# Attention loop of the mixers: probabilities scaled on GpSimd, one turned tile copied by VectorE

## The reference

```python
def attend_latent(q, k, v, k_ctx, v_ctx):          # 256 own tokens, keys: own + context = 512
    k_all = jnp.concatenate([k, k_ctx], axis=1)
    v_all = jnp.concatenate([v, v_ctx], axis=1)
    def one_block(q_blk):                           # 128 queries
        s = jnp.einsum('bqkgd,bskd->bkgqs', q_blk, k_all).astype(jnp.float32) * ATTN_SCALE
        p = jax.nn.softmax(s, axis=-1).astype(v_all.dtype)
        return jnp.einsum('bkgqs,bskd->bqkgd', p, v_all)

def attend_context(q, k, v):                        # layer 0 only: 256 context tokens and keys
    s = jnp.einsum('bqkgd,bskd->bkgqs', q, k).astype(jnp.float32) * ATTN_SCALE
    p = jax.nn.softmax(s, axis=-1).astype(v.dtype)
    return jnp.einsum('bkgqs,bskd->bqkgd', p, v)

for layer in range(2):
    # x, ctx: feed-forward 1; projections; attention, pooling and Fourier mixers, then w_out;
    # feed-forward 2 (the context's last steps only in layer 0)
```

## Time and profile before

| | |
|---|---|
| median of 3 runs | 2139.98 us |
| span of the profiled execution, first to last instruction | 2137.7 us |
| around the span (median less span) | 2.3 us |
| TensorE busy | 2051.8 us, 96% of the span |
| VectorE busy | 1423.7 us, 67% |
| ScalarE busy | 693.6 us, 32% |
| GpSimd busy | 244.5 us, 11% |
| attention loop of layer 0 | about 989.8 to 1038.2 us |
| attention loop of layer 1 | about 1875.4 to 1907.1 us |

### The profile page before, as it was taken

One profiled execution on the slowest core, in us unless ns is written; L12 is line 12 of the kernel. 1 busy time (PEld: TensorE's weight loads), 2 busy tenths in 40 slices (PEclk: granted clock), 3 DMA queues, 4 the chain that ended last, 5 costly groups with the idle time before them and its releaser, 6 DMA issues.

```text
span 2137.7 us, 31334 instructions
## 1 busy us (share of the span) xinstructions
PE 2051.8 (96%) x13199; PEld 1702.5 (80%) x13199; DVE 1423.7 (67%) x1890; ACT 693.6 (32%) x962; POOL 244.5 (11%) x286
## 2 busy tenths in 40 slices
PE   8999988887999999999999999999999999999998
PEld 7988975554888888896798888889888888877887
DVE  6887553333788598356578758747866863767675
ACT  6554421112421221245532112123221222464453
POOL 1000003321200000400210000030000004010000
PEclk9999999999999999999999999999999999999999
DMA  9646769999666565332136456445645643415664
GB/s 278 208 169 207 238 255 385 413 406 400 198 177 183 151 198 163 102 99 65 40 109 198 140 156 180 123 121 153 190 134 164 183 122 118 138 46 153 172 185 121
DMA packets 384121, 387.14 MB, mean 181 GB/s; under 512 B 18041, under 2 KB 351342, under 8 KB 371566
## 3 DMA queue, kind: packets, MB, share of 16 engines
q1 hardware_dynamic: 355438, 304.31, 44.1%
q0 software_dynamic: 27952, 79.77, 12.1%
q10 hardware_dynamic: 592, 1.05, 0.1%
HBM read 430.68 MB, written 1.05 MB: 202 GB/s over the span
## 4 chain that ended last, share of the span: by engine, by line
PE 84%; DVE 7%; DMA 6%; ACT 2%; issue 1%; SPq 0%; POOL 0%; DVEq 0%; POOLq 0%; ACTq 0%
PE B L2020 22%; PE B L2022 22%; PE B L2021 22%; PE B L2525 6%; DMA WB<-in_w 5%; PE B L2526 3%; PE B L2473 3%; DVE LO L816 2%; PE B L2862 1%; PE B L2507 1%; DVE HF L1195 1%; PE B L2836 1%; PE B L2847 1%; DMA W<-in_w 1%; DVE hL L1183 1%
## 5 line engine op out<-in xcount | busy, mean ns | idle before, releaser
L2020 PE MATMUL B<-hH,HI 128*128 128x512 f32 (+1 forms) x1600 | 566.5, 354 | 4.9 <-DVE hL L1183 2.4
L2021 PE MATMUL B<-hL,HI 128*128 128x512 f32 (+1 forms) x1600 | 558.5, 349 | 0.0
L2022 PE MATMUL B<-hH,LO 128*128 128x512 f32 (+1 forms) x1600 | 558.3, 349 | 0.0
L816 DVE TENSOR_TENSOR LO<-RAW,HI 128x2048 fp32r<-128x2048 f32 (+3 forms) x218 | 443.2, 2036 | 94.2 <-ACT HI L1571 89.3
L1571 ACT ACTIVATE HI<-RAW 128x2048 fp32r<-128x2048 f32 (+3 forms) x218 | 368.6, 1693 | 342.0 <-PE B L2022 282.6
L2020 PEld LDWEIGHTS B<-hH,HI 128*128 128x128 f32 x1600 | 302.3, 189 | 49.7 <-DVE LO L816 5.4
L2022 PEld LDWEIGHTS B<-hH,LO 128*128 128x128 f32 x1600 | 302.3, 189 | 40.2
L2021 PEld LDWEIGHTS B<-hL,HI 128*128 128x128 f32 x1600 | 302.3, 189 | 39.6 <-issue 1.2
L904 DVE SCALAR_TENSOR_TENSOR MACC<-MADW,CS,MACC 128x1024 f32<-128x1024 f32 x224 | 277.5, 1280 | 7.7 <-DMA MADW<-in_ada_w 1.7
L2022 PE MATMUL B<-aH,LO 128*128 128x512 f32 (+1 forms) x605 | 222.9, 368 | 0.0
L2020 PE MATMUL B<-aH,HI 128*128 128x512 f32 (+1 forms) x605 | 222.6, 368 | 0.0
(11 more groups left out here) (425 smaller groups left out, 3163.0 us busy)
## 6 DMA issues: line engine op xcount, KB each, us to landing
RAW<-in_ffn_w_gu SPq DMA_DIRECT2D x176, 512.0 KB, 5.3
MADW<-in_ada_w POOLq DMA_DIRECT2D x128, 512.0 KB, 4.0
W<-in_w SPq DMA_DIRECT2D x31, 1024.0 KB
RAW<-in_w_in SPq DMA_DIRECT2D x60, 512.0 KB, 4.8
WB<-in_w SPq DMA_DIRECT2D x28, 1024.0 KB
RAW<-in_ffn_w_down SPq DMA_DIRECT2D x56, 384.0 KB, 3.7
RAW<-in_ffn_w_down SPq DMA_DIRECT2D x56, 320.0 KB, 4.3
WA<-in_w SPq DMA_DIRECT2D x17, 1024.0 KB
```

The costliest lines, as they stand in the source:

```text
L816: V.tensor_tensor(LO[s][:, :words], RAW[s][:, :words], HI[t.hi[s]][:, :words].bitcast(F32), ALU.subtract).then_inc(lo_done[s], 1)
L2020: mm(o, wh, xh, start=first, stop=False, **more)
L2021: mm(o, wh, xl, start=False, stop=False, **more)
L2022: return mm(o, wl, xh, start=False, stop=last, **more)
```

## The change

Three things are done in both layers' attention loops.

1. The scaling of the probabilities leaves VectorE. A new function `probabilities(l)` on GpSimd waits for the reciprocals of a pair (`qr_ready`), multiplies its two tiles in place, and raises `prob_ready`, for which TensorE's transposes wait as before. VectorE no longer waits for its own reciprocals.
2. The copy of the second head's turned probabilities (bank 3 into T3) leaves ScalarE. VectorE does it at the head of its iteration, ahead of the maxima. It waits for both heads' transposes.
3. TensorE waits for two semaphores in place of one count: `probT_ready` of ScalarE and `turned_ready` of VectorE, ahead of the values product and where it reuses the banks.

```diff
+            def probabilities(l):
+                t.n["qr_ready"] += 3 if l == 0 else 2
+                for n, (h, q0, k0, nk) in enumerate(attention_pairs(l)):
+                    pool.wait_ge(E["qr_ready"], t.next("qr_ready"))
+                    for c in range(2):
+                        e = PROBS[2 * n % 6 + c][:, :nk]
+                        i = 4 + 2 * n % 4 + c
+                        ins = nc.gpsimd.tensor_scalar(e, e, SM2[:, i:i + 1], None, ALU.mult)
+                    ins.then_inc(E["prob_ready"], 1)
...
             mod_weights(units[1], units[1] + 2)
+            probabilities(0)
             even_squares_in_turn()
...
             after_ffn(2)
+            probabilities(1)
             even_squares(1)
...
                 for u in range(len(pairs) + 3):
                     i = 2 * u % 4
+                    if u >= 3:
+                        h, q0, k0, nk = pairs[u - 3]
+                        ve.wait_ge(E["probT_done"], t.next("probT_done", 2))
+                        V.tensor_copy(T[3][:, :nk], B[3][:, :nk]).then_inc(E["turned_ready"], 1)
...
                         ve.wait_ge(E["exp_ready"], t.next("exp_ready", 2))
-                        link(V.reciprocal(ri, sums))
-                        for c in range(2):
-                            e = PROBS[2 * (u - 1) % 6 + c][:, :nk]
-                            ins = V.tensor_scalar(e, e, ri[:, c:c + 1], None, ALU.mult)
-                        ins.then_inc(E["prob_ready"], 1)
+                        V.reciprocal(ri, sums).then_inc(E["qr_ready"], 1)
...
-                        for c in range(2):
-                            got("probT_done")
-                            A.activation(T[2 + c][:, :nk], B[2 + c][:, :nk], ACT.Copy).then_inc(E["probT_ready"], 1)
+                        got("probT_done")
+                        t.next("probT_done")
+                        A.activation(T[2][:, :nk], B[2][:, :nk], ACT.Copy).then_inc(E["probT_ready"], 1)
...
-                            claim(2 + c, "probT_ready", before + 2 * (u - 3) + c + 1)
+                            claim(2 + c, *(("probT_ready", before + u - 2), ("turned_ready", before_turned + u - 2))[c])
...
-                        pe.wait_ge(E["probT_ready"], t.next("probT_ready", 2))
+                        got("probT_ready")
+                        got("turned_ready")
                         claim(4, "mix_ready")
```

More of the change, by code:

```diff
@@ L1469, in mixers @@
                 pairs = attention_pairs(l)
+                if l == 0:
+                    t.n["probT_done"] += HEADS
                 for u in range(len(pairs) + 3):
                     i = 2 * u % 4
+                    if u >= 3:
+                        h, q0, k0, nk = pairs[u - 3]
+                        ve.wait_ge(E["probT_done"], t.next("probT_done", 2))
+                        V.tensor_copy(T[3][:, :nk], B[3][:, :nk]).then_inc(E["turned_ready"], 1)
                     if u < len(pairs):
@@ L2827, in mixers @@
                 pairs = attention_pairs(l)
-                before = t.n["probT_ready"]
+                if l == 0:
+                    t.n["turned_ready"] = QUADS
+                t.n["qr_ready"] += len(pairs)
+                before, before_turned = t.n["probT_ready"], t.n["turned_ready"]
                 for u in range(len(pairs) + 3):
```

## The result

The changed kernel takes 2154.14 us (median of 5 runs, 2153.7 to 2155.9) against 2139.98 (2139.85 to 2141.91 in 5 runs). The ratio is 1.0064, 95% interval 1.0053 to 1.0075: slower, by some 14 us, well beyond the 0.2% that a measurement tells. The forecast was 2141.1 and the range ended at 2149.0.

The account below looks back on a forecast made before the run. TensorE's own work was taken as the bound; terms 1.04 + 1.08 + 0.40 - 1.44 = +1.1 us turned the span of 2137.7 into 2138.8, with the median 2.3 above it: 2141.1 us. The range was 2139.3 to 2149.

Parts of the forecast that it names:

- What bounds the kernel, and the room of 2.46 us: Steady 512-key loop: TensorE's own work bounds; from reciprocals to transposes 2.46 us, so GpSimd scalings up to 1.12 us are free.
- The scaling on GpSimd: what one costs: One GpSimd scaling in the attention loops: 0.66 us for 512 columns, 0.42 for 256, from AFFINE_SELECT; upper end 1.29.
- Term 1, the first pair: Start of each layer's loop: transposes wait for GpSimd's two scalings, 0.52 us later per layer, +1.04 us.
- Term 2, the copy on VectorE: Values products without long scores before them: VectorE's copy allows T+2.04 against T+1.83, T being the transposes' start; +1.08 us.
- Term 3, 256 keys: 256-key iterations: VectorE's copy puts the values product at T+1.27 against T+1.22, 0.05 for each of eight pairs, +0.40 us.
- Term 4, the low part sooner: VectorE without scaling writes the low part right after the reciprocals, removing TensorE's waits for it; -1.44 us.
- The sum: Both attention loops: 1.04 + 1.08 + 0.40 - 1.44 = +1.1 us, giving 2141.1 us.
- The first: Rival: GpSimd's scaling bounds the loops from 1.12 us; at 1.29 us 2146.3 us, at 1.6 +12.6, at 2.0 +22.6; chance 0.21.
- The mutual blocking: Rival: VectorE and GpSimd hold each other up in the loops; +4.2 us over the forecast, 2145.3 us; chance 0.05.
- The quick handovers: Rival: freed engines win more than handovers cost in the loops; sum -0.2 to -0.8 us, down to 2139.2; chance 0.10.

Follow-up runs that it names:

- f9: Kernel before, scaling still on VectorE, with GpSimd running scaling, product and copy forms on unused tiles from layer 0's loop on; one run, 2143.3 us.
- f6: The whole change, but GpSimd scales by a product with the reciprocal's column broadcast; ratio to before 1.0005, both loops 81.47 us against 80.11.
- f8b: The whole change plus two filler matmuls on TensorE ahead of each layer's first transposes; ratio to before 1.0051, both loops 92.23 us.
- f7: Kernel before, but GpSimd scales only each layer's first pair, one signal after its two tiles; ratio to before 1.0036, both loops 87.25 us.
- f8: The whole change plus five filler matmuls on TensorE ahead of each layer's first transposes; ratio to before 1.0072, both loops 95.13 us.
- g10: Kernel before, but VectorE writes the low part ahead of the scaling; ratio to before 0.9992, both loops 78.43 us against 80.11.
- f1: Kernel before, only the scaling moved to GpSimd, one signal for a pair's two tiles; ratio to before 1.0063, both loops 93.67 us.
- e1: Kernel before, only the scaling moved to GpSimd, with a signal after every tile; ratio to before 1.0035, both loops 87.82 us.
- e7: Kernel before, but GpSimd scales only each layer's first pair, with a signal after every tile; ratio to before 1.0016, both loops 83.16 us.

## Why the prediction was wrong

*What bounds the kernel, and the room of 2.46 us.* Right. With 1.04 us for a scaling the beats are 3.11, with 1.56 they are 3.50. The rule (each 512-key beat grows by t - 1.12) gives +0.44 at 1.56; measured is +0.39.

*"The scaling on GpSimd: what one costs".* This step failed: 0.66 us was put for an instruction that takes 1.56, and 1.12 is where GpSimd begins to decide. I took 0.66 us from AFFINE_SELECT because it has the scaling's traffic, one read and one write. Runs f9 and f6 show that traffic isn't what GpSimd's time goes by here: 1.67 us with a column, 1.62 with a constant, 1.09 with two inputs, all over the same 512 columns. With the product's 1.04 us in its place, 13.2 of the 14.54 us are gone. The upper bound of 1.29 was no bound, since no row had this form. The Trainium skill, "GPSIMD Engine Reference", section Key points, gave an estimate of 0.88 by its factor of two; measured is 3.5 times VectorE's 0.44, so rule and estimate were both too low.

*Term 1, the first pair.* Its form was right. With t = 1.56 it gives 0.52 + 2 x 0.90 = 2.32 us later per layer (measured 2.27 and 2.24), with 1.04 it gives 1.28 (measured 1.16 and 1.17 in f6). What was missing from the whole text is what TensorE's clock does after such an idle time: +4.17 us in the first beats, of which later beats give 0.5 back (f8b: 3.66 net). It is shown by f7, where nothing else is changed, and by f8 and f8b, where the fillers keep the clock up.

*Term 2, the copy on VectorE: +1.08.* Too high. The last pair of layer 1 has the copy at T+1.13 and the values product at T+1.92, not T+2.04 (T+1.83 before). The copy begins 0.08 us sooner than I put it, and the handover takes 0.10, not 0.14 (the row's bracket names ScalarE, whose copy ended at 1919.86; VectorE's ended last, at 1920.39):

```profile
1918.57 1.09 PE L2854 MATMUL B<-MATS,T 128*128 128x128 f32 x8
...
1919.70 0.69 DVE L1490 COPY T<-B 128x512 f32<-128x512 f32 x1 [0.55 <-PE B L2854]
...
1920.49 1.09 PE L2881 MATMUL B<-T,VD 128*64 128x128 f32 x16 [0.83 <-ACT T L1956]
```

*Term 3, 256 keys: +0.40.* Near nothing by itself: the last values product of layer 0 comes at T+1.22 (1043.64 to 1044.86 after), as an undisturbed one did before. f6 stands 3.04 us above g10, 2.33 of it at the start; so by subtraction the terms 2 and 3 were worth 0.7 together, not 1.48.

*Term 4, the low part sooner: -1.44.* Right: -1.68, measured by itself in g10.

*The sum.* With the measured 1.04 us of the product, start +2.33, terms 2 and 3 +0.7, term 4 -1.68: +1.36, the loops of f6 (from which the 0.7 was taken, so this is no test of the sum). That it lies near the forecast's +1.1 is in part luck: at 1.04 us term 1 as recorded gives +2.56 and the whole sum +2.6. What f6 does show is that with a scaling of 1.04 us the kernel stays within the range.

*The rivals.* The first was what happened, at 0.21 the likeliest of the three. Two of its figures don't follow from its own steps. With 0.18 us fixed, 1.6 us means 0.89 at 256 keys: 4.8 for ten beats, 3.8 for the starts, 2.2 for the 256-key beats and the forecast's 1.1 make +11.8, not +12.6; at 2.0 us they make some +18.8, not +22.6. The mechanism without the clock gave 14.54 - 3.66 = 10.9 at 1.56 us, near the +11.8; the whole is above it for lack of the clock. The mutual blocking was no cause here: in layer 0 VectorE's reciprocals have a median of 158 ns beside GpSimd (159 before), with the longest of 16 at 410, and GpSimd's scalings a mean of 1.56 us. But it is real, as f9 shows, once VectorE scales tiles in SBUF beside GpSimd. The quick handovers were partly right (T+1.92), and worth nothing beside the rest.

The range failed with the same step: 2154.14 lies above its end at 2149. I priced an instruction that no row showed from its neighbours and gave 0.79 to its being under a threshold at 1.12 us, with a nearby row at 1.29.

## What to carry to other kernels

On GpSimd the instruction's form matters more than its traffic: time the very form before moving it there, and try a product with a broadcast column in place of a scaling by a scalar. Where an engine has a threshold within reach of the price's uncertainty, the chance belongs on both sides of it. A signal after each part of a result, in place of one after the last, may be worth more than it looks: here 5.85 us, as the first transposes wait in two short pieces and not in one long one. A wait of about 2 us ahead of TensorE may cost twice, once as idle time and once as the slower matmuls after it; look at the granted clock in short stretches.

## What the runs showed of the hardware that was not expected

- GpSimd, 128x512 float32: TENSOR_SCALAR 1.56 us (the change), TENSOR_TENSOR 1.04 to 1.09 (f6, f9). At 256 columns 0.92 and 0.61, COPY 0.40.
- An idle time of 2.20 us of TensorE was followed by 3 to 7 us at the lower clock level (score matmuls of 1.22 us for 0.69) in both layers of every kernel with it: the change, f1 and f7 (granted clocks of 0.66 to 0.77 in the 5 us in which it fell; the duration is worked out from them). Ahead of it stood a shorter wait, 0.56 us in layer 0 and 1.20 in layer 1, which the kernel before has too. After 1.10 us (f6) the clock stayed. With two waits of 0.66 and 0.89 us it fell in e1's layer 0 (0.77 from 1000 to 1005 us), and neither in e1's layer 1 nor in e7.
- A VectorE scaling of two 128x512 tiles in SBUF took up to 1.99 us for 0.88 beside a busy GpSimd. The Trainium skill, "SBUF — State Buffer", section "SBUF: two separate sides", describes such a lock, held for a whole instruction. The two scalings that make up the 1.99 us end 0.28 us after the GpSimd instructions that ran beside them, at 1003.73 and 1004.90, which agrees. In the 1.32 us pair the second ended at 998.06, while GpSimd's scaling (996.89 to 998.66) still ran, which does not; times on GpSimd are rough.
